# Keys' and queries' norms by column quarter: packed sums of squares, a short root and reciprocal, four spreading matmuls

## The reference, cut to what matters

```python
def rms_norm(x, g):
    y = x * rsqrt(mean(x * x, axis=-1, keepdims=True) + EPS)
    return y * g

q    = rms_norm(q_a, q_a_norm_g) @ w_q_b                    # 384 -> 8 heads x (64 + 32)
c_kv = rms_norm(kv_a[..., :256], kv_a_norm_g)               # then @ w_kv_b: keys and values
```

## Time and profile before

| | us |
|---|---|
| median of 3 runs | 1242.41 (1241.79 to 1242.85) |
| profiled execution | 1243.72 |
| its span | 1241.9 |
| PE busy | 1209.8 |
| VectorE busy | 851.4 |
| ScalarE busy | 517.1 |
| GpSimd busy | 41.8 |
| mean granted TensorE clock | 0.997 |

### The profile page before, as it was taken

How to read it: one execution, slowest core, us unless ns; L and a number is a source line. 1 busy time by engine, 2 the same in 40 slices (tenths; PEclk the granted TensorE clock), 3 DMA queues, 4 the chain that set the end, 5 groups by cost and what they waited for, 6 DMA issues and landing times.

```text
span 1241.9 us, 18361 instructions
## 1 busy us (share of the span) xinstructions
PE 1209.8 (97%) x7194; PEld 1022.7 (82%) x7194; DVE 851.4 (69%) x1301; ACT 517.1 (42%) x850; POOL 41.8 (3%) x44
## 2 busy tenths in 40 slices
PE   7999999999999999999999999999999999999997
PEld 6767777687887888888888888888879999999996
DVE  4664666768777478678755665789788877655555
ACT  4432555522433353222232223465665555544443
POOL 0000000000000200000000000300000002000000
PEclk9999999999999999999999999999999999999999
DMA  9838412134454526547664654335444574766662
GB/s 303 266 113 248 107 53 68 35 84 121 116 165 126 169 80 191 170 143 216 185 200 148 213 192 148 103 85 148 118 122 107 155 211 137 205 188 187 187 185 85
DMA packets 265254, 188.92 MB, mean 152 GB/s; under 512 B 16035, under 2 KB 250833, under 8 KB 265169
## 3 DMA queue, kind: packets, MB, share of 16 engines
q1 hardware_dynamic: 264832, 187.60, 51.5%
q10 hardware_dynamic: 337, 0.15, 0.0%
HBM read 186.67 MB, written 1.05 MB: 151 GB/s over the span
## 4 chain that ended last, share of the span: by engine, by line
PE 83%; DVE 7%; ACT 3%; issue 2%; DMA 1%; SPq 0%; DVEq 0%; ACTq 0%
PE bank L1950 20%; PE bank L1952 20%; PE bank L1951 20%; PE scores L2383 2%; DVE Wlo L406 2%; PE bank L2363 2%; PE bank L2365 2%; PE bank L2364 2%; PE probsT L2392 2%; ACT Whi L395 1%; PE attended L2406 1%; DVE RSTD L1327 1%; PE bank L2462 1%; PE bank L2464 1%; PE bank L2463 1%
## 5 line engine op out<-in xcount | busy, mean ns | idle before, releaser
L406 DVE TENSOR_TENSOR Wlo<-Wraw,Whi 128x1024 fp32r<-128x1024 f32 (+3 forms) x294 | 314.7, 1077 | 132.3 <-ACT Whi L395 131.3
L1950 PE MATMUL bank<-Hhi,Whi 128*128 128x512 f32 (+1 forms) x1114 | 379.3, 341 | 3.2 <-DVE Wlo L406 3.1
L1951 PE MATMUL bank<-Hlo,Whi 128*128 128x512 f32 (+1 forms) x1114 | 374.8, 336 | 0.0
L1952 PE MATMUL bank<-Hhi,Wlo 128*128 128x512 f32 (+1 forms) x1114 | 374.7, 336 | 0.0
L395 ACT ACTIVATE Whi<-Wraw 128x1024 fp32r<-128x1024 f32 (+1 forms) x296 | 270.9, 928 | 152.1 <-PE bank L1952 72.2
L1950 PEld LDWEIGHTS bank<-Hhi,Whi 128*128 128x128 f32 x1114 | 211.5, 190 | 33.2 <-issue 7.0
L1951 PEld LDWEIGHTS bank<-Hlo,Whi 128*128 128x128 f32 x1114 | 211.5, 190 | 22.8 <-issue 1.2
L1952 PEld LDWEIGHTS bank<-Hhi,Wlo 128*128 128x128 f32 x1114 | 211.5, 190 | 22.0
L1950 PE MATMUL bank<-Uhi,Whi 128*128 128x512 f32 (+1 forms) x350 | 127.8, 365 | 0.0
L1952 PE MATMUL bank<-Uhi,Wlo 128*128 128x512 f32 (+1 forms) x350 | 126.7, 362 | 0.0
L1951 PE MATMUL bank<-Ulo,Whi 128*128 128x512 f32 (+1 forms) x350 | 126.6, 362 | 0.0
(11 more groups left out here) (274 smaller groups left out, 1664.3 us busy)
## 6 DMA issues: line engine op xcount, KB each, us to landing
Wraw<-in_w_ff SPq DMA_DIRECT2D x126, 512.0 KB, 4.0
Wraw<-in_w_in SPq DMA_DIRECT2D x78, 512.0 KB, 4.0
ATT<-in_w_mod SPq DMA_DIRECT2D x58, 512.0 KB, 4.5
Wraw<-in_w_o SPq DMA_DIRECT2D x16, 512.0 KB, 4.3
ACC<-in_w_mod SPq DMA_DIRECT2D x14, 512.0 KB, 4.6
Wraw<-in_w_mla_o SPq DMA_DIRECT2D x8, 512.0 KB, 3.4
ATT<-in_w_mod SPq DMA_DIRECT2D x12, 256.0 KB, 6.3
Wraw<-in_w_kv_b SPq DMA_DIRECT2D x12, 256.0 KB, 4.0
```

Of the source, the lines that this page charges most:

```text
L406: last = eng.tensor_tensor(lo, raw, hi.bitcast(F32), ALU.subtract)
L1950: pe.matmul(dst, sh, mh, start=j == 0, stop=False)
L1951: pe.matmul(dst, sh, ml, start=False, stop=False)
L1952: last = pe.matmul(dst, sl, mh, start=False, stop=j == k - 1)
```

## The change

The sums of squares of keys and queries are no longer spread over 128 partitions by the sum itself. Each column quarter g (128 or 64 columns) is summed into 32 partitions, 32g to 32g + 31, by a 128x32 block of ones: eight matmuls per sum, into bank S[1] outside the ring. ACT takes the root and DVE the reciprocal of a quarter of the columns on all 128 partitions. Then four matmuls with the selectors `PICK[:, g, :]` (row 32g is ones) spread the quarters to all partitions, into PV for the keys and PT for the queries, and `normed` reads the factor there. The keys' spread stands on PE behind P6, the queries' behind P8 (and its mod steps). The chunk that DVE and ACT split behind the normed queries (chunk 11) is split ahead of them. The ring has two tiles fewer.

```diff
+        def packed(what, n):
+            a = what * P
+            return slice(a, a + n // 4), slice(2 * P + a, 2 * P + a + n // 4)
+        SPREAD = [PV, PT]
...
+            v = mark(pool.memset(PICK[:, :, :], 0.0))
+            pool.wait_ge(pool_step, v)
+            for g in range(4):
+                pool.memset(PICK[32 * g:32 * g + 1, g, :], 1.0).then_inc(selector, 1)
+                pool.wait_ge(selector, g + 2)
...
+            def packed_root(l, what, n, width):
+                here, _ = packed(what, n)
+                act.wait_ge(stat_sum, 2 * l + what + 1)
+                act.activation(ROOT[:, here], S[1][:, here], ACT.Sqrt, bias=EPS, scale=1.0 / width).then_inc(root_done, 1)
...
                     if j == 0:
-                        root(T, KVL)
+                        packed_root(l, 0, T, KVL)
...
                 copy_out(TG[:, 1, 0:TQ], TQ, ACT.Tanh, 0.5)
-                root(TQ, QL)
+                packed_root(l, 1, TQ, QL)
                 for k in range(2):
                     operand(Uhi[:, CT0 + k, :], Z[:, k % 2, :])
+                step_in()
                 for k in range(3):
                     operand(Uhi[:, QT + k, 0:TQ], Z[:, k % 2, 0:TQ])
                 glu = []
                 for j in range(2):
-                    step_in()
+                    if j:
+                        step_in()
...
+            def packed_inverse(l, what, n):
+                here, to = packed(what, n)
+                dve.wait_ge(root_done, stat_root(l, 1 + what))
+                dve.reciprocal(ROOT[:, to], ROOT[:, here]).then_inc(inverse_done, 1)
...
-            def normed(l, n, tiles, raw0, to, gain):
+            def normed(l, n, tiles, raw0, to, gain, what):
+                dve.wait_ge(stat_spread, 2 * l + what + 1)
...
-                                             PAR[:, l, gain + k:gain + k + 1], RSTD[:, 0:n],
+                                             PAR[:, l, gain + k:gain + k + 1], SPREAD[what][:, 0:n],
...
                 step_in()
-                take_root(T, stat_root(l, 1), of_keys)
+                packed_inverse(l, 0, T)
                 keep_raw(4, TQ)
                 step_in()
                 tanh_g.append(at.tile())
-                normed(l, T, 2, 0, CT0, KVG)
-                take_root(TQ, stat_root(l, 2))
-                normed(l, TQ, 3, 2, QT, QG)
+                normed(l, T, 2, 0, CT0, KVG, 0)
+                packed_inverse(l, 1, TQ)
+                step_in()
+                normed(l, TQ, 3, 2, QT, QG, 1)
                 for j in range(2):
-                    step_in()
+                    if j:
+                        step_in()
...
+            def packed_total(what, n, count):
+                here, _ = packed(what, n)
+                c, last = n // 4, (at.square.n - 1) % 2
...
+                for src, end in ((first, False), (SQ[:, last, :], True)):
+                    if end:
+                        pe.wait_ge(sq_done, at.square.n)
+                    for g in range(4):
+                        ins = pe.matmul(S[1][32 * g:32 * (g + 1), here], ONES[:, 0:32], src[:, g * c:(g + 1) * c],
+                                        start=not end, stop=end)
+                ins.then_inc(stat_sum, 1)
+            def spread(l, what, n):
+                _, at_inverse = packed(what, n)
+                c = n // 4
+                pe.wait_ge(inverse_done, 2 * l + what + 1)
+                pe.wait_ge(selector, 5)
+                if what:
+                    pe.wait_ge(mod_done, at.turn)
+                for g in range(4):
+                    ins = pe.matmul(SPREAD[what][:, g * c:(g + 1) * c], PICK[:, g, :], ROOT[:, at_inverse],
+                                    start=True, stop=True)
+                ins.then_inc(stat_spread, 1)
...
                 projection(TQ)
-                total(T, 2)
+                packed_total(0, T, 2)
                 for _ in range(2):
                     projection(TQ)
+                spread(l, 0, T)
                 at.square.n += 3
                 projection(TQ)
-                total(TQ, 3)
-                for _ in range(8):
+                packed_total(1, TQ, 3)
+                for i in range(8):
                     projection(TQ)
+                    if i == 0:
+                        spread(l, 1, TQ)
```

More of the change, by code:

```diff
@@ L220, in build @@
         ROWSEL = sb("ROWSEL", [P, 64])
+        PICK = sb("PICK", [P, 4, P])
         PAR = sb("PAR", [P, 4, P])
@@ L286, in build @@
         x_norm = sem("x_norm")
+        stat_sum = sem("stat_sum")
+        inverse_done = sem("inverse_done")
+        stat_spread = sem("stat_spread")
         shared_in = sem("shared_in")
@@ L1500, in _ @@
                 step_in()
-                of_keys = at.tile()
                 keep_raw(3, TQ)
                 step_in()
-                take_root(T, stat_root(l, 1), of_keys)
+                packed_inverse(l, 0, T)
                 keep_raw(4, TQ)
@@ L2159, in total @@
                           start=False, stop=True).then_inc(tile_done, 1)
+            def packed_total(what, n, count):
+                here, _ = packed(what, n)
+                c, last = n // 4, (at.square.n - 1) % 2
+                if count > 2:
+                    at.added.n += count - 1
+                    pe.wait_ge(sq_summed, at.added.n)
+                    first = SUM
+                else:
+                    pe.wait_ge(sq_done, at.square.n - 1)
+                    first = SQ[:, 1 - last, :]
+                for src, end in ((first, False), (SQ[:, last, :], True)):
[16 more added lines that the diff above has]
+                ins.then_inc(stat_spread, 1)
             def mod_step():
```

## The result

| | before | after |
|---|---|---|
| median of 6 runs, us | 1242.28 (1241.79 to 1243.07) | 1251.54 (1251.00 to 1252.75) |
| ratio, 95% interval | | 1.0072 (1.0062 to 1.0081) |
| profiled execution, us (span) | 1243.72 (1241.9) | 1251.00 (1249.2) |

A forecast was written before the change was run, and what follows sets the result against it. TensorE (PE) was taken to bound the kernel. Layer 0's +2.96, layer 1's +1.70 and 3.0 for two clock falls gave +7.7 on the median 1242.41: 1250.1 us, range 1245.8 to 1252.2.

The forecast's parts named there:

- Part 1: Sums on PE: 0.78 us each in quarters, 0.94 saved per sum at 512 columns; layer 1's query sum 0.65.
- Part 2: Spreads on PE: 0.99 us behind a wait, 0.89 without, for 128 columns; 0.60 for layer 1's 64-column one.
- Part 3: VectorE's reciprocals: 0.96 us for 128 columns, 0.56 for 64; nothing counted for products reading the factor from PSUM.
- Part 4: Layer 0: PE stalls 4.1 us before the keys' spread, second reciprocal hides; +2.96 us in all.
- Part 5: Layer 1: PE stalls 3.5 us before the keys' spread, 1.27 before the queries'; chunk 11's wait goes, 1.34; +1.70 us.
- Part 6: PE's clock falls behind each of the two long stalls, costing 1.5 us each, between 0 and 1.7.
- The sum: Whole kernel: 2.96 + 1.70 + 3.0 = +7.7 us, giving 1250.1; chance of this forecast 0.52.
- A: Layer 0 stretch, keys' sum to third pair of mod steps; forecast terms 2.96 plus 1.5 us for the clock.
- B: Layer 1 stretch, an earlier sum of squares to first product with normed keys; forecast terms 1.70 plus 1.5 us.
- the reciprocal in time: Rival: both spreads pass without a wait, 1237.9 us; chance 0.07 at both places, 0.05 at one.
- Stalls without the clock's fall: Rival: both layers' waits cost, the clock holds: +4.7 us, 1247.1; chance 0.30 for clock at one place or none.
- Quarters one after another: Rival: PE's sum quarters don't run beside each other, near 1254 us; chance 0.06, shared with an unseen cost.

The follow-up runs named there:

- e3_fill: Changed kernel with idle matmuls of ones filling PE's waits before the keys' spreads in both layers: ratio 1.0027 to the kernel before.
- e5_keys_late: Changed kernel with the keys' spread moved behind the queries' sum in both layers: ratio 0.9967 to the kernel before.
- e2_order_undone: Changed kernel with chunk 11 split behind the queries' operands again, as before the change: ratio 1.0067 to the kernel before.
- e6_both_late: Changed kernel with the keys' spread behind the queries' sum in both layers and layer 1's queries' spread behind P9: ratio 0.9962 to the kernel before.
- e8_own_banks: Kernel before, with full-width sums in banks of their own, a second root buffer and chunk 11 split earlier; no spreads: ratio 0.9977 to the kernel before.
- e1_order_alone: Kernel before, with only chunk 11's split moved ahead of the queries' operands: ratio 0.9990 to the kernel before.
- e0_changed_again: The changed kernel run once more, nothing edited: ratio 1.0065 to the kernel before.
- e4_keys_late_l0: Changed kernel with the keys' spread moved behind the queries' sum in layer 0 alone: ratio 1.0010 to the kernel before.

## Why the prediction was right

The mechanism, its two places and the time came as forecast. By its steps:

- **Part 1, sums.** 60.37 to 61.60 less two steps of 0.23: 0.77, forecast 0.78. With 64-column quarters 851.72 to 852.52 less 0.24: 0.56, at the low end of what I had given (0.65 taken).
- **Part 2, spreads: one term was wrong.** The 128-column one was given 0.89 without a wait, 0.99 with one, and took 0.81 to 0.92 (e3_fill, e5_keys_late) at full clock. The 64-column one was given 0.60, "time still follows columns". It took 0.92 behind the wait (856.32 to 857.24) and 0.81 without one. Halving the columns saves nothing. This is the rule of the Trainium skill (TensorE: Matmul & The Clock Gate, LDWEIGHTS) that I had set against my reading, and it held: by it I had put the spread at about 0.86, an estimate, and these runs show 0.81 to 0.92 for either width. My row of three 95-column instructions was too thin to overrule it. It isn't of the spread's kind: L2274 makes three transposes, one instruction each, where each product of the spread is two; its operand was 95 rows high, not 128; and its 0.08 a step came out of a difference of two small numbers, one of them a tail. Which of these made the steps shorter wasn't tried.
- **Part 3, reciprocals.** 0.94 and 0.55, forecast 0.96 and 0.56:

```profile
845.65 0.94 DVE L1357 RECIPROCAL ROOT<-ROOT 128x128 f32<-128x128 f32 x1
...
855.72 0.55 DVE L1357 RECIPROCAL ROOT<-ROOT 128x64 f32<-128x64 f32 x1
```

- **Part 4, layer 0.** Forecast wait 4.1, measured 3.90. The chunk's split and so the reciprocal moved with the mod steps, the second spread found its factor ready.
- **Part 5, layer 1.** Forecast 3.5 and 1.27; measured 846.65 - 843.00 - 0.12 = 3.53 and 856.32 - 855.14 - 0.12 = 1.06. The wait for chunk 11 went away, but not because of the new order, as I had it: e2_order_undone does without it too. PE's delay alone hides the split. The sum didn't depend on which.
- **Part 6, clock.** Forecast 1.5 and 1.5, isolated by e3_fill 1.72 and 1.33.
- **The sum.** A: 2.96 + 1.5 = 4.46 forecast, 4.23 measured. B: 1.70 + 1.5 = 3.20 forecast, 3.12 measured. In B the 64-column spread cost 0.3 more, and the shorter second wait and sum 0.3 less: two errors that happened to cancel. The measured medians differ by 9.3 where 7.7 was forecast, so the result is in the upper part of the range. The steps add up to 7.35, 0.3 less than forecast; the other 2 us are in no step of the sum. Single executions differ by that much (start-up, length of the low clock), and one profile of each kernel doesn't show which of these it was. The range's upper bounds, by the terms that it names, add up to 1252.0 and not 1252.2; the result is below both.

Of the rivals, the one that would be faster (the reciprocal in time, 1237.9) is what e6_both_late makes of the kernel: 0.9962 times the median of the 6 runs before, 1242.28, is 1237.6. The rival had the price of a missing wait right, and the wrong point in PE's order for this kernel. *Stalls without the clock's fall* is e3_fill: 1.0027, or +3.4 us, and +4.3 in A and B, where +4.7 was worked out. *Quarters one after another* is excluded by the 16 instructions' 0.65 us: one after another they were to take 1.7.

## What to carry to other kernels

A shorter chain on the side engines only helps if the place where PE picks up its result isn't moved ahead by more than the chain was cut. Here 2.4 us came off a reciprocal, and PE's first instruction that waits for it was put a whole tile earlier (5.5 us in layer 0, 2.9 in layer 1, where the reciprocal's start hardly moved). List for each wait when its releaser is done, and place the waiting instruction behind that; moving the keys' spread was worth 0.6% in layer 0 and 0.4% in layer 1, and turned +0.7% into -0.3%. And ask which half of a change gains: three quarters of what the best order of the change gains in A and B (3.1 of 4.1 us) is there with banks of their own and chunk 11's new place alone (e8_own_banks), which need no new arithmetic. Each of the two waits of 3.5 to 3.9 us cost about 1.5 us more than itself by the clock, and matmuls that do no work bought that back.

## What the runs showed of the hardware that I had not expected

- The 128x64 spread costs as much as the 128x128: 0.81 us for eight instructions in both without a wait, 0.92 in both behind one. The number of columns that stream, 64 or 128, doesn't matter to it.
- The clock's fall is not settled by the length of the wait alone. Behind a wait of 1.93 us it held in the kernel before and behind the same one of 1.92 us it fell in e1_order_alone, with PE's busy time over those 14 us equal (12.07 and 12.08); a fall behind the same wait of 3.4 us left 0.88 over 14 us in one profile and 0.76 in another, of the same program. What decides it wasn't found, and no run here was made for it. Behind all seven waits of 3.4 to 3.9 us in the profiles (two each in after, e0_changed_again and e2_order_undone, one in e4_keys_late_l0) the granted clock fell. For a forecast of this kernel that means: a wait near 2 us costs between nothing and about 1.5 us beyond itself, one of 3.4 to 3.9 about 1.5, once some 1.4 more.
